# Gathering the tokens of the experts by halves instead of quarters, and a place of its own for the second layer's first gate matrix

## What is computed

```python
def ec_ffn(h, router_w, w_gate, w_up, w_down):
    cap = EC_CAPACITY_FACTOR * n_tok // N_EXPERTS           # 2 * 256 // 16 = 32
    aff = jax.nn.softmax((h @ router_w).astype(jnp.float32), axis=-1)
    top_aff, idx = lax.top_k(jnp.swapaxes(aff, 1, 2), cap)  # each of 16 experts takes 32 tokens
    xg = jax.vmap(lambda hb, ib: hb[ib])(h, idx)            # the gather
    hid = jax.nn.silu(jnp.einsum('becd,edf->becf', xg, w_gate)) * jnp.einsum('becd,edf->becf', xg, w_up)
    y = jnp.einsum('becf,efd->becd', hid, w_down) * top_aff[..., None].astype(h.dtype)
    return ...  # y scattered back to its tokens and added
```

## Time and profile before

| | us |
|---|---|
| median of 3 runs | 2329.77 (2326.97 to 2331.62) |
| the profiled execution, its time | 2326.75 |
| its span in the trace | 2324.9 |
| PE busy in the span | 2215.8 (95%) |
| DVE busy | 733.0 (32%) |
| ACT busy | 449.6 (19%) |
| bytes moved by DMA | 435.04 MB, mean 187 GB/s |

### The profile page before, as it was taken

The page is one execution under the profiler, slowest core; times in us unless marked ns, Lnnn a source line. Parts: engine busy times, 40 slices in busy tenths (PEclk is TensorE's granted clock), DMA queues, the critical chain, the costliest instruction groups (busy, mean ns, idle before and its releaser), DMA issues.

```text
span 2324.9 us, 27404 instructions
## 1 busy us (share of the span) xinstructions
PE 2215.8 (95%) x11751; PEld 1657.2 (71%) x11751; DVE 733.0 (32%) x1559; ACT 449.6 (19%) x974; POOL 88.6 (4%) x88
## 2 busy tenths in 40 slices
PE   6999999999899999998999999999999998999998
PEld 3444587765565476654878888888888788788887
DVE  2137623122335731112356423200015543141001
ACT  3005422111122420001133112100003421210000
POOL 1000010000000010000001100000000011000000
PEclk9999999999999999999999999999999999999999
DMA  9561504889932449999423214443643222244353
GB/s 372 216 222 42 182 14 202 363 337 424 415 111 73 145 185 390 425 426 415 149 82 113 96 37 145 155 165 107 169 147 138 85 105 73 101 153 145 127 143 93
DMA packets 172905, 435.04 MB, mean 187 GB/s; under 512 B 6218, under 2 KB 64498, under 8 KB 156146
## 3 DMA queue, kind: packets, MB, share of 16 engines
q1 hardware_dynamic: 171648, 430.90, 49.5%
q10 hardware_dynamic: 1138, 2.39, 0.3%
HBM read 432.23 MB, written 1.05 MB: 186 GB/s over the span
## 4 chain that ended last, share of the span: by engine, by line
PE 87%; DMA 5%; DVE 4%; ACT 2%; issue 1%; ACTq 0%; DVEq 0%
PE bank L274 83%; DMA ring<-in_exp_w_up 2%; PE bank L530 2%; PE bank L760 1%; DMA arena<-in_exp_w_up 1%; DMA ring<-in_exp_w_gate 1%; DMA ring<-in_w_in 1%; DMA arena<-in_x 1%; ACT arena L730 0%; DVE arena L725 0%; ACT h L638 0%; ACT h L618 0%; DVE x L1203 0%; PE bank L456 0%; DVE arena L810 0%
## 5 line engine op out<-in xcount | busy, mean ns | idle before, releaser
L274 PE MATMUL bank<-h,ring 128*128 128x256 f32 (+2 forms) x3952 | 936.4, 397 | 13.3 <-ACT arena L584 4.9
L274 PEld LDWEIGHTS bank<-h,ring 128*128 128x128 f32 (+1 forms) x3952 | 750.0, 191 | 185.4 <-issue 78.1
L274 PE MATMUL bank<-arena 128*128 128x128 f32 (+12 forms) x2016 | 363.5, 368 | 26.3 <-issue 9.4
L274 PEld LDWEIGHTS bank<-arena 128*128 128x128 f32 (+5 forms) x2016 | 258.6, 196 | 117.2 <-issue 68.4
L274 PE MATMUL bank<-arena,ring 128*128 128x256 f32 x1216 | 264.9, 379 | 1.0 <-PE bank L274 1.0
L274 PEld LDWEIGHTS bank<-arena,ring 128*128 128x128 f32 x1216 | 230.1, 190 | 33.1 <-PE bank L274 1.8
L730 ACT ACTIVATE arena<-bank 128x256 f32<-128x256 f32 (+5 forms) x263 | 116.2, 461 | 636.9 <-PE bank L274 612.2
L274 PE MATMUL bank<-ring,arena 128*64 128x256 f32 x1376 | 154.7, 380 | 9.0 <-DMA ring<-in_exp_w_up 6.5
L725 DVE COPY arena<-bank 128x256 f32<-128x256 f32 (+7 forms) x114 | 60.9, 535 | 283.8 <-PE bank L274 232.1
L274 PEld LDWEIGHTS bank<-ring,arena 128*64 128x64 f32 x1376 | 100.0, 137 | 68.8 <-DMA ring<-in_exp_w_up 9.5
L597 POOL TENSOR_TENSOR arena<-arena 128x256 f32<-128x256 f32 (+1 forms) x51 | 42.7, 837 | 1556.5 <-ACT arena L584 1290.2
(11 more groups left out here) (306 smaller groups left out, 1571.4 us busy)
## 6 DMA issues: line engine op xcount, KB each, us to landing
ring<-in_w_in SPq DMA_DIRECT2D x31, 2048.0 KB, 7.8
ring<-in_exp_w_gate SPq DMA_DIRECT2D x22, 2048.0 KB, 12.2
ring<-in_exp_w_up SPq DMA_DIRECT2D x21, 2048.0 KB, 10.6
ring<-in_exp_w_down SPq DMA_DIRECT2D x20, 2048.0 KB, 12.5
ring<-in_ada_w SPq DMA_DIRECT2D x18, 2048.0 KB, 10.2
ring<-in_w_ffn_down SPq DMA_DIRECT2D x16, 1408.0 KB, 6.8
ring<-in_w_ffn_gate SPq DMA_DIRECT2D x10, 2048.0 KB, 7.6
ring<-in_w_ffn_up SPq DMA_DIRECT2D x10, 2048.0 KB, 7.7
```

Of the source, the lines that this page charges most:

```text
L274: return PE.matmul(o, lhsT, rhs, start=(k == 0), stop=(k == n - 1))
```

## The change

The gather goes by two halves of the experts. A unit now handles one value of k and 8 experts: two matmuls of 256 columns, and one copy of 256 columns as before. The first half is gathered ahead of expert 0, the second is spread over steps 0 to 9. The comparisons that write `sel` are split 8 and 8 instead of 4 and 12 experts. `sel` is weighted in one piece after step 9 (four operations of 512 columns in layer 0, two in layer 1), and `slots` stands in steps 10 to 13.

In layer 1 the gate matrix of expert 0 is loaded to a new place, `SPLIT_SLOT`: its first four k in the last 2048 columns of the arena, the other four in the half of `x` that holds the residual of the context. SP issues it in two loads, after the last `ada_w` matrix has been read. The other matrices of the layer shift by one place.

```diff
+            last_ada = len(stream) - 1
...
-                run_chunk(l, A["exp_w_gate"][l, e], KD, FF)
+                run_chunk(l, A["exp_w_gate"][l, e], KD, FF, l == L - 1 and e == 0)
...
+        low_half = arena[:, AR - 4 * FF:AR].rearrange("p (k n) -> p k n", k=4)
+
+        def load_split(sp, n):
+
+            src = stream[n][0]
+            sp.dma_start(low_half, src[:, 0:4, :]).then_inc(loaded[SPLIT_SLOT], 16)
+            sp.dma_start(x[:, :, S:T2], src[:, 4:KD, :].rearrange("p k (h n) -> p (k h) n", h=2)).then_inc(loaded[SPLIT_SLOT], 16)
...
-            return [(q, u // 4, 2 * (u % 4)) for q, (first, last) in enumerate(GATHER_AT, 1) for u in spread(4 * NS, first, last, n)]
+            return [divmod(u, KD) for u in spread(KD * NS, 0, LAST_GATHER, n)]
...
-        GATHER_AT, SCATTER_AT = [(0, 4), (5, 9), (10, 14)], ((12, 16), (17, 24), (25, 31))
+        LAST_GATHER, SLOTS_AT, SCATTER_AT = 9, 10, ((12, 16), (17, 24), (25, 31))
-
-        def gather_tensor(pe, l, s, k, q):
-            b = take(pe, "xg", l, s, k, q)
-            for i in range(2):
-                for j in range(2):
-                    last = mm(b[:, i * P:(i + 1) * P], htok[:, 2 * s + j, k + i:D:KD],
-                              sel[l][s][j][:, 4 * q:4 * q + 4, :].rearrange("p e c -> p (e c)"), j, 2)
-            last.then_inc(*tensor.mark("xg", l, s, k, q))
+        def gather_tensor(pe, l, s, k, half):
+            b = take(pe, "xg", l, s, k, half)
+            for j in range(2):
+                last = mm(b[:, 0:S], htok[:, 2 * s + j, k:D:KD], sel[l][s][j][:, 8 * half:8 * half + 8, :].rearrange("p e c -> p (e c)"), j, 2)
+            last.then_inc(*tensor.mark("xg", l, s, k, half))
...
-            if e in (4, 8, 12):
-                for k in (KD - 4, KD - 2):
-                    pe.wait_ge(*got("xg", l, NS - 1, k, e // 4))
+            if e == 8:
+                for k in (KD - 2, KD - 1):
+                    pe.wait_ge(*got("xg", l, NS - 1, k, 1))
...
-            for part, (e0, e1) in enumerate(((0, 4), (4, NE))):
+            for half in range(2):
...
+                    if home[n] == SPLIT_SLOT:
+                        wait_used(last_ada)
+                        for s in (tensor, scalar, vector):
+                            value = s.closed(("in", L - 1))
+                            if value:
+                                sp.wait_ge(*value)
+                        load_split(sp, n)
+                    else:
+                        load(n)
```

More of the change, by code:

```diff
@@ L209, in program @@
         gpsimd = Signals("gpsimd", nc, ctx, book)
-        loaded = [sem(f"slot_loaded_{i}") for i in range(RING + 3)]
+        loaded = [sem(f"slot_loaded_{i}") for i in range(RING + 4)]
         const_loaded, cond_loaded, tokens_loaded, vec_loaded, rest_loaded, late_loaded, second_loaded, stored = (
@@ L339, in w_chunk, with run_chunk @@
             settle([*range(RING)] + [CONST_SLOT] * first_block[0])
-        def run_chunk(l, src, k, n):
+        def run_chunk(l, src, k, n, split=False):
             stream.append((src.rearrange("(p k) n -> p k n", p=P), k, n))
-            settle([*range(RING), CONST_SLOT] + [SPARE_SLOT] * (l == L - 1))
+            settle([SPLIT_SLOT] if split else [*range(RING), CONST_SLOT] + [SPARE_SLOT] * (l == L - 1))
         IN1 = [(1312, 1824), (928, 1312), (0, 416), (416, 928)]
@@ L1206, in between_tensor @@
             NS = 2 if l < L - 1 else 1
[L1207 to L1210, removed]
+            for s, k in late_gather(l, n):
+                gather_tensor(pe, l, s, k, 1)
+            if 0 <= n - SLOTS_AT < 4:
+                g = n - SLOTS_AT
+                pe.wait_ge(*vector.at("weighted", l, NS - 1, 1))
                 b = take(pe, "slots", l, g)
@@ L1225, in between_vector @@
             NS = 2 if l < L - 1 else 1
[L1226 to L1230, removed]
+            for s, k in late_gather(l, n):
+                if k % 2 == 0:
+                    out_vector(dve, *gather_out(l, s, k, 1), "xg", l, s, k, 1)
+            if n == LAST_GATHER:
+                dve.wait_ge(*tensor.at("xg", l, NS - 1, KD - 1, 1))
                 for s in range(NS):
                     for j in range(2):
-                        a = sel[l][s][j][:, 4 * q:4 * q + 4, :]
-                        V.tensor_tensor(a, a, aff[:, j, s, 4 * q:4 * q + 4].unsqueeze(2).broadcast_to((P, 4, CAP)), ALU.mult)\
-                         .then_inc(*vector.mark("weighted", l, s, j, q))
+                        V.tensor_tensor(sel[l][s][j], sel[l][s][j], aff[:, j, s, :].unsqueeze(2).broadcast_to((P, NE, CAP)), ALU.mult)\
+                         .then_inc(*vector.mark("weighted", l, s, j))
             for g, s, d in early_scatter(l, n):
@@ L1240, in between_scalar @@
             NS = 2 if l < L - 1 else 1
[L1241 to L1244, removed]
+            for s, k in late_gather(l, n):
+                if k % 2:
+                    out_scalar(act, *gather_out(l, s, k, 1), "xg", l, s, k, 1)
+            if 0 <= n - SLOTS_AT < 4:
+                g = n - SLOTS_AT
                 out_scalar(act, scat[l][:, 0:NS, g, :], bank("slots", l, g)[:, 0:NS * S].rearrange("p (s t) -> p s t", s=NS), "slots", l, g)
@@ L1365, in moe_tensor @@
                 pe.wait_ge(*vector.at("sel", l, s, 0))
-                for k in range(0, KD, 2):
+                for k in range(KD):
                     gather_tensor(pe, l, s, k, 0)
@@ L1414, in moe_vector @@
             dve.wait_ge(*vector.now("posT"))
-            for part, (e0, e1) in enumerate(((0, 4), (4, NE))):
+            for half in range(2):
                 for s in range(NS):
                     for j in range(2):
-                        V.tensor_tensor(sel[l][s][j][:, e0:e1, :],
-                                        posT[l][:, j, s, e0:e1].unsqueeze(2).broadcast_to((P, e1 - e0, CAP)),
-                                        C("slots").unsqueeze(1).broadcast_to((P, e1 - e0, CAP)), ALU.is_equal).then_inc(*vector.mark("sel", l, s, part))
+                        V.tensor_tensor(sel[l][s][j][:, 8 * half:8 * half + 8, :],
+                                        posT[l][:, j, s, 8 * half:8 * half + 8].unsqueeze(2).broadcast_to((P, 8, CAP)),
+                                        C("slots").unsqueeze(1).broadcast_to((P, 8, CAP)), ALU.is_equal).then_inc(*vector.mark("sel", l, s, half))
             for s in range(NS):
-                for k in range(0, KD, 4):
+                for k in range(0, KD, 2):
                     out_vector(dve, *gather_out(l, s, k, 0), "xg", l, s, k, 0)
@@ L1449, in moe_scalar @@
             for s in range(NS):
-                for k in range(2, KD, 4):
+                for k in range(1, KD, 2):
                     out_scalar(act, *gather_out(l, s, k, 0), "xg", l, s, k, 0)
@@ L2561, in _ @@
                                 sp.wait_ge(*value)
-                    load(n)
+                    if home[n] == SPLIT_SLOT:
+                        wait_used(last_ada)
[6 more added lines that the diff above has]
+                        load(n)
                     if n == LATE_AT:
```

23 lines of the change are left out of this document (12 added, 11 removed).

## The result

The changed kernel takes 2308.27 us (median of 4, 2306.86 to 2312.37) against 2330.69 of the kernel before beside it (4, 2326.97 to 2333.82): a ratio of 0.9907, 95% interval 0.9887 to 0.9927. That is 22.4 us less where 24 were forecast; the interval goes from 17 to 26 us, so it doesn't tell these two apart. The profiled execution is the slowest of its four (2312.37), and that of before (2326.75) is faster than all four beside it, so the two traces lie only 14.3 us apart.

What follows compares the result with a forecast made beforehand. Layer 0's experts were taken as bound first by PE, then by weight loads, layer 1's by weights nearly throughout. 22.4 us (layer 0) plus 1.5 (layer 1) made 24, from 2329.8 to 2305.8, stated as 2305.5; range 2297 to 2318.

Steps and rivals of the forecast that it cites:

- The record's pace: Gather on PE: the strided stationary load sets 0.24 us a record, also at 256 columns; bounds 0.223 to 0.48.
- the 6 records in one us: Layer 1's first gather: 6 records start in 1 us at half clock, as at full clock, so columns hide.
- Rival (a): Gather: load and matmul one after the other, 0.345 us a wide record; gain only 10 us, 2320; 8 in 100.
- rival (b): Gather: time goes by columns, 0.48 us a record; 13 us slower, 2343; 4 in 100.
- The queue in layer 0: Layer 0: earlier issue of expert 3's gate matrix keeps weight loads following at 4.92 us; gives 22.4 us.
- the 8.3 us from the issue to the landing of gate matrix 3: Layer 0: time a load with nothing ahead of it takes to land, giving 408.4 + 8.3 = 416.7.
- The 1.3 us allowed for the pace: Layer 0: allowance for loads not quite keeping 4.92 us, from layer 1's 1084.6 against 1085.88; 23.7 becomes 22.4.
- the split place frees nothing: Layer 1: the next load still waits for up matrix 0's read, so the queue stands empty the same few us.
- Rival (c): Layer 1 gives a whole matrix, 4.9 us, and the DMA dip, 2.4 us: 29 us in all, 2300; 10 in 100.
- The 1.5 us: Layer 1's total gain: 2.3 us from earlier loads against 1.3 us for the low clock; range 0.5 to 2.3.
- the low clock: Layer 1's first gather: at half clock a 256-column record takes about 0.43 us, costing 1.3 us once.
- the earlier start of the full queue: Layer 1: queue full from expert 2's down matrix, last landing 1083.6 against 1085.88; 2.3 us.

Runs made afterwards that it cites:

- e4: Kernel before, gather still by quarters, no split place, with `htok` written so the gather's stationary operand is dense: 2295.15 us, ratio 0.9847.
- e5: Changed kernel (halves and split place) with `htok` written so the gather's stationary operand is dense: 2305.03 us, ratio 0.9891.
- e10: Kernel before with `htok` written so the gather's stationary operand has a step of 8 bytes: 2292.2 us in one execution, beside 2333.29.
- e2: Changed kernel without the split place, the gather by halves kept: 2307.94 us, ratio 0.9902.
- e3: Kernel before with the split place alone, the gather by quarters: 2329.9 us, ratio 0.9998.
- e6: Changed kernel with the split place used twice in layer 1, for the gate matrices of experts 0 and 2: 2303.96 us, ratio 0.9882.
- e12: Kernel of e10 plus the split place, used for the gate matrices of experts 0 and 2 of layer 1: 2293.35 us, ratio 0.9836.
- e1: The changed kernel once more, against the kernel before: 2308.04 us, ratio 0.9905.
- e9: Kernel before with `htok` written so the gather's stationary operand has a step of 16 bytes: 2326.84 us in one execution, beside 2333.29.

## Why the prediction was right

**The record's pace, forecast 0.24, measured 0.244.** The strided weight load hides the width. e4, e5 and e10 show the cause by taking the step away: the record falls to 0.114 for 128 columns and 0.218 for 256. One of the forecast's readings was wrong, though its conclusion holds: the 6 records in one us of the earlier trace rows are those that lie in it at least in part, not those that start. From 863.3 to 866.8 the clock is at 0.50 and the narrow records start 0.238 us apart, some 4 in 1 us, as at full clock.

Rival (a), load and matmul in turn, would have made the wide record 0.345; rival (b), 0.48. Both fall. With the layout of e5, a dense load of about 190 ns with 256 columns runs at 0.218, so it lies beside the matmul: from 0.114 to 0.218 the record grows by 0.104 for 128 columns more, which leaves 0.010 us for a load in turn. The rule of the Trainium skill (TensorE: Matmul & The Clock Gate, Part 3, The mechanism) that a load overlaps with matmuls in flight only when the row group differs doesn't hold for these full-height operands.

**The queue in layer 0.** Issue of gate matrix 3 forecast at 408.4, measured 408.9; queue full from about 410, in the windows from 412; last up matrix to land at 598.7 + 1.3 = 600.0, its read starts at 604.15 - 2.95 = 601.2. The stage gave 21.2 for a forecast 22.4. The term that was too small is the 8.3 us from the issue to the landing of gate matrix 3, the shortest time of the earlier trace rows: in the times of the trace before it landed at 419.05, 10.2 us after its issue. The pace was as forecast: the last up matrix lands at 601.16, 182.1 us later, for 37 x 4.92 = 182.0. The 1.3 us allowed for the pace weren't needed there and covered a part of the 1.9 us that the landing took longer.

**Layer 1.** That the split place frees nothing is shown by e2 and e3. Rival (c), a whole matrix gained, falls; a part of it comes when a second matrix takes the place (3.0 us in e6, 3.8 in e12). The 1.5 us were right in the first profile (1.4) by luck, two errors that met: there the low clock was absent, so that 2.3 should have come. With the low clock (1.5 us of cost in e1, forecast 1.3) the stage gave 0.2 in e1 and 0.1 in e2. The down matrix of expert 3 shows that it is the clock: it lands 66.4 us after the anchor in the profile after, 67.7 in e1 and in e2, and the last up matrix lands 1.2 us later than in the profile after in both.

The step that was mis-sized is the earlier start of the full queue, 2.3 forecast; measured 1.4 without the low clock, and 0.2 + 1.5 = 1.7 in e1 with its cost added back. The forecast took an issue ahead of the end of the queue to be as good as a full queue. In the profile after, the up matrix of expert 3 was issued 51.9 us after the anchor (forecast 51.4), 2.9 us before the matrix ahead of it landed, and it landed at 61.5, 9.6 us after its issue; the forecast's terms make it 60.2. From there to the landing of the last up matrix it is 178.1 us in both kernels. The end of the queue at 898.7 doesn't follow from the forecast's own terms (895.3 + 4.92 = 900.2).

The split load was forecast near 772 and came at 785.49. The forecast took the row for the read of the last `ada_w` matrix, but in the timeline of PE of the kernel before another one follows:

```profile
800.02 1.92 PE L530 MATMUL bank<-ring,arena 128*32 128x512 f32 x16
```

Nothing hangs on it: the matrix landed 35 us before the anchor.

**The sum**: 24 forecast, 22.4 and 22.2 measured in the medians. Nearly all of the 15 us of PE time taken out of layer 1, and some 10 of layer 0's 31, stand as waits for weights. What stood outside the forecast is the clock in stretches without changed work; they are 8.2 us longer in the profiled execution, more than layer 1 gave.

## What to carry to other kernels

When a short float32 matmul runs slower than its columns, look at the duration of its weight loads before making the matmuls wider: here a layout with a step of at most 8 bytes gave 35 us where halving the number of records gave 22. In a stage that becomes bound by loads, PE time counts in full only ahead of the point where the queue is full, so shorten what stands before the first consumer and not what is spread later. A place for an earlier load gains nothing unless the matrix behind it can also move up; follow what the next waiting load waits for.

## What the runs showed of the hardware

- The load of a 128x128 float32 stationary operand takes 192 ns with neighbouring elements, 197 at a step of 8 bytes, 328 at 16 and 334 at 32, as the profiler records it. These records overlap; the records of 128 columns start 0.112, 0.118, 0.233 and 0.240 us apart. The jump lies between 8 and 16 bytes, and nothing between them was run. The Trainium skill (SBUF — State Buffer, the note on cachelines in Door 1: The DMA port swizzle) has 4 fp32 as a stride for free; at a step of 4 fp32 e9 measured the full cost. What the same note of the Trainium skill says ahead of that figure, that full bandwidth needs at least two hits in a line of 16 bytes, agrees with e9 and e10: a step of 16 bytes has one element in a line, one of 8 bytes two. The limit of 8 bytes that the Trainium skill's GPSIMD Engine Reference, section 7, gives for reads by that engine lies in the same interval as the jump of TensorE's weight loads.
- ACT's copy of 128x512 out of PSUM took 602 ns written side by side, 612 ns in pairs of neighbours with the pairs 1 KB apart (e10), and 1067 ns with neighbours 512 bytes apart (e4).
- At the 1.2 GHz level the narrow strided record kept its 0.24 us (0.238 in the kernel before, 863.3 to 866.8) while the wide one did not (0.427 in e1 and e2): 3.4 us at the low clock cost the gather 1.5 us in e1. Here the width was hidden only at full clock.
- A load that was issued shortly before the queue ran empty landed later than the shortest of the earlier trace rows would have it, 8.3 us: 10.2 us after its issue in layer 0 and 9.6 in layer 1. Behind it the full queue kept 4.92 us a matrix in layer 0 (37 matrices in 182.1 us) and 4.95 in layer 1 (36 in 178.1).
